# A decoder block on one core: x also read transposed, mixer weights in pieces in their order of use, no transposes ahead of the first product

## The reference

```python
def reference(x, p, positions, g_mix_norm, w_in, ...):
    h = rms_norm(x, g_mix_norm[i])
    proj = h @ w_in[i]
    q, k, v, g_ret, u_pool, gate_a, gate_b = jnp.split(proj, ...)
    qh = rotary(q.reshape(B, S, RET_HEADS, RET_HEAD_DIM), positions)
    kh = rotary(k.reshape(...), positions) * (RET_HEAD_DIM ** -0.5)
    ret = retention_chunkwise(qh, kh, vh)
    ...
    merged = jax.nn.sigmoid(gate_a) * branch_a + jax.nn.sigmoid(gate_b) * branch_b
    x = x + merged @ w_out[i]
    h2 = rms_norm(x, g_ffn_norm[i])
    x = x + moe(h2, w_router[i], b_router[i], w_gate_up[i], b_gate_up[i], w_down[i], b_down[i])
    h3 = rms_norm(x, g_ple_norm[i])
    ple_gate = jax.nn.sigmoid(h3 @ w_ple_gate[i])
    x = x + ple_gate * (p[i].astype(x.dtype) @ w_ple_proj[i])
    return rms_norm(x, g_final)
```

## Time and profile before

| | before |
|---|---|
| median of 3 runs | 1224.1 us (1223.71 to 1224.15) |
| span of the profiled execution, first to last instruction | 1221.4 us |
| TensorE busy | 1143.5 us, 94% |
| VectorE busy | 392.4 us, 32% |
| ScalarE busy | 202.4 us, 17% |
| moved by DMA | 457.25 MB, mean 374 GB/s |
| chain that ended last | TensorE 62%, DMA 33%, VectorE 3% |

### The profile page before, as it was taken

How to read it: one execution, slowest core, us unless ns; L and a number is a source line. 1 busy time by engine, 2 the same in 40 slices (tenths; PEclk the granted TensorE clock), 3 DMA queues, 4 the chain that set the end, 5 groups by cost and what they waited for, 6 DMA issues and landing times.

```text
span 1221.4 us, 12440 instructions
## 1 busy us (share of the span) xinstructions
PE 1143.5 (94%) x5360; PEld 588.4 (48%) x5361; DVE 392.4 (32%) x619; ACT 202.4 (17%) x273; POOL 8.4 (1%) x19
## 2 busy tenths in 40 slices
PE   7999999999999999989898988989999779989887
PEld 6788888874344343424342434343443344343336
DVE  6964765641132121303030403131302121221226
ACT  6464545430000010101010101010100000000115
POOL 0000010000000000000000000000000000000000
PEclk9999999999999999999999999999999989999999
DMA  9855345898999999999999999999999999999990
GB/s 346 317 173 170 114 168 206 357 427 367 399 420 427 428 428 428 428 429 428 427 427 428 428 423 428 428 427 427 427 428 428 429 425 427 427 429 425 421 372 35
DMA packets 57500, 457.25 MB, mean 374 GB/s; under 512 B 5466, under 2 KB 6874, under 8 KB 30370
## 3 DMA queue, kind: packets, MB, share of 16 engines
q1 hardware_dynamic: 55632, 453.26, 89.7%
q10 hardware_dynamic: 1810, 3.14, 0.8%
HBM read 455.34 MB, written 1.05 MB: 374 GB/s over the span
## 4 chain that ended last, share of the span: by engine, by line
PE 62%; DMA 33%; DVE 3%; issue 1%; ACT 0%; SPq 0%; DVEq 0%; ACTq 0%; POOLq 0%; POOL 0%
PE ps L674 61%; DMA ring<-in_w_down 27%; DMA ring<-in_w_gate_up 5%; DVE w_split L1481 1%; PE ps L681 1%; PE ps L982 0%; DMA const<-in_const 0%; PE ps L999 0%; DVE over_xn L1489 0%; SPq L627 0%; DVE ring L1773 0%; DVE ring L1536 0%; DVE B L1719 0%; DVE B L1723 0%; DVE B L1720 0%
## 5 line engine op out<-in xcount | busy, mean ns | idle before, releaser
L674 PE MATMUL ps<-ring,B 128*64 128x512 f32 (+1 forms) x2976 | 659.4, 597 | 50.3 <-DMA ring<-in_w_gate_up 34.2
L674 PEld LDWEIGHTS ps<-ring,B 128*64 128x64 f32 (+1 forms) x2976 | 226.7, 140 | 468.3 <-issue 463.7
L1719 DVE TENSOR_SCALAR B<-ps 128x1024 f32<-128x1024 f32 x16 | 19.6, 1225 | 462.1 <-PE ps L982 379.7
L674 PE MATMUL ps<-w_split,over_BhT 128*128 128x512 f32 x480 | 152.3, 393 | 0.9 <-DVE ring L1540 0.8
L1481 DVE TENSOR_TENSOR w_split<-ring,w_split 128x1024 fp32r<-128x1024 f32 x87 | 104.7, 1223 | 67.8 <-ACT w_split L1224 67.3
L1224 ACT CAST w_split<-ring 128x1024 fp32r<-128x1024 f32 x87 | 90.4, 1052 | 101.6 <-PE ps L674 99.0
L674 PE MATMUL ps<-w_split,over_xn 128*128 128x512 f32 x256 | 100.0, 390 | 0.0
L674 PEld LDWEIGHTS ps<-w_split,over_BhT 128*128 128x128 f32 x480 | 90.0, 189 | 19.9 <-DVE ring L1540 1.2
L1350 ACT COPY B<-ps 128x512 f32<-128x512 f32 x28 | 15.0, 588 | 508.4 <-PE ps L982 508.4
L674 PE MATMUL ps<-const,xn 128*128 128x128 f32 x512 | 61.6, 279 | 4.1 <-DVE const L1688 3.6
L674 PEld LDWEIGHTS ps<-const,xn 128*128 128x128 f32 x512 | 60.0, 196 | 6.8 <-issue 6.8
(11 more groups left out here) (166 smaller groups left out, 495.4 us busy)
## 6 DMA issues: line engine op xcount, KB each, us to landing
ring<-in_w_gate_up SPq DMA_DIRECT2D x118, 2048.0 KB, 32.4
ring<-in_w_down SPq DMA_DIRECT2D x56, 2048.0 KB, 31.8
ring<-in_w_in SPq DMA_DIRECT2D x28, 1024.0 KB, 5.4
ring<-in_w_gate_up SPq DMA_DIRECT2D x18, 1024.0 KB, 11.5
ring<-in_w_down SPq DMA_DIRECT2D x16, 1024.0 KB, 25.5
ring<-in_w_branch SPq DMA_DIRECT2D x8, 1024.0 KB, 6.9
ring<-in_w_out SPq DMA_DIRECT2D x4, 1024.0 KB, 5.0
ring<-in_w_ple_gate SPq DMA_DIRECT2D x4, 1024.0 KB, 19.9
```

Of the source, the lines that this page charges most:

```text
L674: return pe.matmul(out, lhsT, rhs, start=start, stop=stop, skip_group_check=True)
L1719: step(ve.tensor_scalar(gate, two_banks(0), LIMIT, None, ALU.min))
```

## The change

- x is handed over a second time, already transposed (`in_xT`, laid out as 128 partitions x 8 column blocks x 256 tokens), and loaded in four parts of 256 KB into the buffer B3. `high_x` and `low_x` make the two parts of hT from it in SBUF; the transposes of x and the banks that they filled are gone.
- `vectors` is handed over as 50 columns of 128 rows, loaded straight into `vecs`; the transposes and copies of the vectors are gone. The cast of the positions moves behind the low part of piece 5.
- The mixer's weights and the gate's come as one tensor `in_mixer` of 45 chunks, each laid out as its slot is, so that a chunk is 8 KB in a row per partition where it was four runs of 2 KB. Chunk 0 comes in two halves, between the parts of xT.
- x itself, which is still needed for the norm and the residual, is loaded behind chunk 2.
- For the first piece, TensorE goes through both token tiles column by column of h, with a wait for each ingredient (`first_products`).
- VectorE clears a block of 128x128 and TensorE multiplies it by itself eight times into an otherwise idle bank before the first product.

```diff
+            load_xT(0)
+            sp.dma_start(ring[:, 0, 0:PIECE], t["mixer"][0, :, 0:PIECE]).then_inc(first_half_loaded, 16)
+            load_xT(1)
+            sp.dma_start(ring[:, 0, PIECE:], t["mixer"][0, :, PIECE:]).then_inc(mixer_loaded[0], 16)
+            load_xT(2)
+            load_xT(3)
+            for c in range(1, 3):
+                load(c)
             for i in range(TILES):
                 sp.dma_start(x[:, i, :], t["x"][0, i * P:(i + 1) * P, :]).then_inc(x_loaded[i], 16)
-
-            w_in = t["w_in"][0].rearrange("(k p) n -> p k n", p=P)
...
+            for c in range(3, MIXER_CHUNKS):
+                load(c)
...
-            pe.wait_ge(early_loaded, 16)
-
-            pe.wait_ge(vec_loaded, 16)
-            pe.transpose(ps[:, 0, 0:5 * KD], vec_rows, ident[0:5 * KD, 0:5 * KD])
...
-            for i in range(TILES):
-                pe.wait_ge(x_loaded[i], 16)
-            for j in range(4):
-                transpose_bank(x, 4 + j, j, xT_psum)
+            pe.wait_ge(blank_ready, 1)
+            for _ in range(WARM_UP):
+                mm(ps[:, 6, 0:P], blank, blank, True, True)
...
+            e.wait_ge(vec_loaded, 16)
+            e.wait_ge(xT_or_gate_loaded[0], 16)
+            high_x(0)
             piece_loaded(e, 0)
             nc.scalar.copy(split_of(0)[:, 0, 0:N], piece_of(0)[:, 0:N]).then_inc(first_hi, 1)
+            high_x(1)
             nc.scalar.copy(split_of(0)[:, 0, N:], piece_of(0)[:, N:]).then_inc(hi_ready, 1)
             split[0] = 1
             for part in range(1, PARTS):
-                high(hT_parts, xT_psum, 0, G_MIX, hT_hi, 4, range(2 * part, 2 * part + 2))
+                e.wait_ge(xT_or_gate_loaded[part], 16)
+                for c in (2 * part, 2 * part + 1):
+                    high_x(c)
+                if part == 1:
+                    e.wait_ge(mixer_loaded[0], 16)
                 split_hi(part + 1)
...
             split_lo(ahead(-1))
+            step(ve.tensor_copy(pos, pos_int))
+            dve.wait_ge(early_loaded, 16)
...
-            w_gate = t["w_ple_gate"][0].rearrange("(k p) n -> p k n", p=P)
...
+            for at, unit in enumerate(PLE_RAW):
+                sp.wait_ge(used, RING.raw_free[at])
+                sp.dma_start(ring[:, unit, :], t["mixer"][MIXER_CHUNKS + at]).then_inc(xT_or_gate_loaded[at], 16)
```

More of the change, by code:

```diff
@@ L327, in build @@
         more = ExpertSemaphores(sem, "more")
+        more.pair_done, more.order = sem("more_pair_done"), sem("more_order")
         used = first.chunk_used
@@ L333, in build @@
         last_rows = sem("last_rows")
-        gate_loaded = [sem(f"gate_loaded{i}") for i in range(len(PLE_RAW))]
+        xT_or_gate_loaded = [sem(f"xT_or_gate_loaded{i}") for i in range(PARTS)]
         block = ctx.enter_context(nc.Block())
@@ L503, in load, with load_xT @@
                         sp.wait_ge(lo_ready, 2 * (former - (former > POOL_CHUNK)) + 2)
-                dst = ring[:, c % MIXER_SLOTS, :].rearrange("p (k n) -> p k n", k=k)
-                sp.dma_start(dst, src).then_inc(mixer_loaded[c % MIXER_SLOTS], 16)
+                sp.dma_start(ring[:, c % MIXER_SLOTS, :], t["mixer"][c]).then_inc(mixer_loaded[c % MIXER_SLOTS], 16)
+            def load_xT(part):
+                sp.dma_start(xT[:, 2 * part:2 * part + 2, :], t["xT"][:, 2 * part:2 * part + 2, :]).then_inc(xT_or_gate_loaded[part], 16)
+            load_xT(0)
[6 more added lines that the diff above has]
+                load(c)
             for i in range(TILES):
                 sp.dma_start(x[:, i, :], t["x"][0, i * P:(i + 1) * P, :]).then_inc(x_loaded[i], 16)
-            w_in = t["w_in"][0].rearrange("(k p) n -> p k n", p=P)
[L511 to L529, removed]
+            for c in range(3, MIXER_CHUNKS):
+                load(c)
             def load_fine(unit):
@@ L691, in transpose16, with products @@
                     transpose_bank(src, 4 + j, j, done)
-            def products(piece, part, i, parts, n_bank, halves=None):
+            def products(piece, part, i, parts, n_bank):
                 hi, lo = parts
@@ L1491, in low, with low_x @@
                                                  ALU.mult, ALU.subtract), done)
-            low(hT_parts, G_MIX, hT_hi, 0, hT_ready, 4, range(0, 2))
-            for columns, after, done in ((slice(0, N), first_hi, first_lo), (slice(N, 2 * N), hi_ready, lo_ready)):
+            def low_x(c):
+                dve.wait_ge(hT_hi, c + 1)
+                post(ve.scalar_tensor_tensor(hT_parts[1][:, c, :], xT[:, c, :], vecs[:, G_MIX + c:G_MIX + c + 1],
+                                             hT_parts[0][:, c, :].bitcast(F32), ALU.mult, ALU.subtract), hT_ready)
+            for c, after, done in ((0, first_hi, first_lo), (1, hi_ready, lo_ready)):
+                columns = slice(c * N, (c + 1) * N)
+                low_x(c)
                 dve.wait_ge(after, 1)
@@ L1499, in _ @@
             for part in range(1, PARTS):
-                low(hT_parts, G_MIX, hT_hi, 0, hT_ready, 4, range(2 * part, 2 * part + 2))
+                for c in (2 * part, 2 * part + 1):
+                    low_x(c)
                 split_lo(part + 1)
             split_lo(ahead(-1))
+            step(ve.tensor_copy(pos, pos_int))
+            dve.wait_ge(early_loaded, 16)
             for i in range(TILES):
@@ new lines, in vectors, with chunks, halves @@
+    words[:, G_HG:G_HG + KD] = by_row.transpose(1, 0, 2).reshape(P, KD)
+    words[:, POSITIONS:] = np.asarray(inputs["positions"][0], np.int32).reshape(TILES, P).T
+    return words.view(np.float32)
+def chunks(inputs):
+    import numpy as np
+    def halves(w, columns):
+        block = w.reshape(2, KD // 2, P, -1)[:, :, :, columns]
+        return [half.transpose(1, 0, 2).reshape(P, SLOT) for half in block]
+    w_in, w_branch, w_out, w_gate = (np.asarray(inputs[n][0]) for n in ("w_in", "w_branch", "w_out", "w_ple_gate"))
+    made = []
+    for j, cb in enumerate(COLUMN_BLOCKS):
+        if j == POOL_AFTER:
+            made.append(np.asarray(inputs["w_pool"][0]).reshape(KD, P, SEQ).transpose(1, 0, 2).reshape(P, SLOT))
+        made += halves(w_in, slice(cb * N, (cb + 1) * N))
+    width = [slice(n * N, (n + 1) * N) for n in range(2)]
+    for unit in range(4):
+        made += halves(w_branch[1 - unit % 2], width[unit // 2])
+    by_width = [halves(w_out, width[n]) for n in range(2)]
+    made += [by_width[n][half] for half in range(2) for n in range(2)]
+    assert len(made) == MIXER_CHUNKS
+    for n in range(2):
+        made += halves(w_gate, width[n])
+    return np.ascontiguousarray(np.stack(made))
@@ L1928 @@
     arrays = {f"in_{n}": np.ascontiguousarray(inputs[n]) for n in _INS}
-    arrays["in_const"], arrays["in_vectors"] = constants(), vectors(inputs)
+    arrays["in_const"], arrays["in_vectors"], arrays["in_mixer"] = constants(), vectors(inputs), chunks(inputs)
+    arrays["in_xT"] = np.ascontiguousarray(inputs["x"][0].T.reshape(KD, P, SEQ).transpose(1, 0, 2))
     tensors = {n[3:]: nc.dram_tensor(n, a.shape, mybir.dt.from_np(a.dtype), kind="ExternalInput").ap()
```

103 lines of the change are left out of this document (48 added, 55 removed).

## The result

| | before | after |
|---|---|---|
| median of ten executions | 1223.74 us (1222.96 to 1224.15) | 1226.95 us (1226.41 to 1228.60) |
| span of the profiled execution | 1221.4 us | 1225.0 us |
| T2 in the profiled execution | 34.84 us | 38.22 us |
| span less T2 | 1186.6 us | 1186.8 us |
| first product | 10.96 us | 7.13 us |

A forecast was written before the change was run, and what follows sets the result against it. The opening's chain through VectorE to T2 was taken as the bound, with chunk 4 just in time. T2 0.5 us later and nothing elsewhere made the span 1221.9, plus 2.7 gave 1224.6 us; range 1221.2 to 1227.8.

The forecast's parts named there:

- T2: Moment VectorE has read column block 0 and TensorE then runs without a gap; forecast to move from 34.84 to about 35.3.
- The forecast's own band: Opening: chunk 4 decides, having been only just in time with a megabyte now ahead; 1223.4 to 1225.9 us, chance 0.42.
- the slower rival: Opening: x starves and TensorE's clock falls at T2; 1226.3 us, with the clock 1228.0; chance 0.22.
- First product at 6.1: TensorE's start: first product at about 6.1 us, 4.8 us earlier, after the first half chunk lands and is cast.
- Blanks 1.8 to 3.7 us from 1.1: TensorE's opening: eight blank matmuls take 1.8 to 3.7 us from about 1.1 us, over before 6.1, costing nothing.
- x at 21.5, scaling at 24.7: Opening: x lands at 21.5 us, between bounds 16.8 and 23.8; VectorE scales sine and cosine at 24.7, before 24.84.
- the rival in which x starves: Part of the slower rival: x lands at 23.8, scaling at 27.0 instead of 24.84, T2 2.2 us later, 1226.3 us.
- The other half of that rival, the clock: TensorE idle 3.6 us before T2, so its clock falls there and adds 1.7 us: 1228.0 us.
- Chunk 4 at 28.1: SP's queue: chunk 4 lands at 28.1 instead of 26.4 us, 2.65 later for x less four times 0.23.
- the rival on the other side: The faster rival: larger packets also fill the biases' slow stretch, giving back 1.0 us, 1223.6 us; chance 0.26 overall.
- No gain by larger packets: SP's queue: larger packets bring no rate, chunk 4 at 29.05, T2 1.4 us later, 1225.5 us; chance 0.1.
- Faster: the DMA keeps up: Opening loads: chunk 4 before 26 us; 1223.6, or 1223.0 down to 1219.3 if VectorE's own work decides; chance 0.26.

The follow-up runs named there:

- f4: Changed kernel with xT in one load and chunk 0 in one load, in place of six pieces: 1227.29 us, ratio 1.0026.
- e5: Kernel before with only the mixer's weights handed over as one tensor in 8 KB rows; x and its transposes as before: 1225.23 us, ratio 1.001.
- e2: Changed kernel with only the expert biases issued after the cosine, the large constants left in place: 1223.46 us, ratio 0.9999.
- e1: Changed kernel with both large constants and expert biases issued on ScalarE's queue after the cosine: 1224.43 us, ratio 1.0008.
- f1: Changed kernel with constants and biases issued behind the cast of piece 9, and VectorE's angles computed between the low parts of pieces 2 to 5: 1220.83 us, ratio 0.9975.
- f2: Changed kernel with VectorE's angles computed between the low parts of pieces 2 to 5, constants and biases where they were: 1226.99 us, ratio 1.0026.
- f3: Changed kernel with WARM_UP at 0, leaving out the eight blank matmuls: 1226.62 us, ratio 1.0023.

## Why the prediction was right, and where it was wrong

The forecast was no change, 1224.6 us; it came out slower, 1226.95, inside the range but past the 2.4 us that I had set as the border, by 0.8 us. **The mechanism held; the size of one term did not.** The move was forecast as 0.5 us and came as 3.2, 2.7 more. In the time itself less of that shows, since the base of 1224.1 was 0.36 above the median of ten; it is not the span plus 2.7 either, for in every execution listed the time is 1.76 to 1.95 above its span.

*The range.* The forecast's own band, 1223.4 to 1225.9, was missed by 1 us. The range took the result in only because it was drawn wide for the slower rival, whose mechanism did not come about: in so far the hit was luck.

*What counts is T2.* Right: the table above. The first product 3.8 us earlier, the blanks and the rest of the mixer left no trace in the end.

*First product at 6.1.* It came at 7.13. The opening moved 0.37 MB less from 3 to 9 us than before (two windows of 280 and 356 GB/s). It cost nothing here, as TensorE had slack. Ahead of chunk 4 stand five more issues of SP and not two, and it is issued at 6.53 instead of 5.5; with the DMA share at 0.97 and 1.02 from 3 to 9 us no cost of that shows.

*Blanks 1.8 to 3.7 us from 1.1.* 3.78 from 1.03, the upper bound.

*x at 21.5, scaling at 24.7.* 21.41 and 24.66. The guess between 16.8 and 23.8 was good, and with it fell the rival in which x starves. The other half of that rival, the clock, fell too: TensorE's idle 3.64 us before piece 6 did lower the granted clock (0.77 on average from 29.8 to 37.2 us), but pieces 6 and 7 still ended 1.08 us before T2, and at T2 the clock was 1.00.

*Chunk 4 at 28.1.* **This is the term that failed**: it landed at 30.84, 2.7 us later. From there on the forecast's own steps hold: 7.2 us from landing to T2 were forecast, 7.4 came. What I had left out, each priced at 424 GB/s:

- The divided opening: 0.37 MB less from 3 to 9 us, 0.9 us. That it goes with the division is shown by f4.
- The stretch of the biases: 0.92 MB less than at 424 GB/s, 2.2 us, where before it was 0.52 MB less than at 388, 1.3 us: 0.9 us more. That this needs no second x is shown by e5. I had priced it only as a gain, in the rival on the other side.
- Bytes that went ahead: 0.93 MB of later chunks before the last byte of chunk 4, where I had kept the 0.35 of before: 0.58 MB, 1.4 us. It stands in e2 too (8.25 MB of SP's queue had moved when chunk 4 landed at 27.5), so it isn't the work of the biases; by f4 and e5 (0.40 and 0.30 MB) it goes with the division of the opening, not with the larger rows. What makes the packets of one load lag so far behind those of the next was not found.

These are 3.2 us, 0.5 more than the miss; by subtraction, the larger rows gave that much beyond the 0.92 us that I had credited them with. One sum checks the whole: by the landing of chunk 4, 10.57 MB had moved instead of 8.97, 1.60 MB more at the same mean rate; nearly all of it x (1.05) and the bytes that went ahead (0.58). At 340 GB/s 1.60 MB are 4.7 us, and chunk 4 was 4.4 later. No run moved x alone, so its share is by bytes and not by a test.

*No gain by larger packets* was the rival that came nearest (chunk 4 at 29.05, 1225.5). It is right for the sum over the opening, 340 against 343 GB/s, but not for its reason: the rows are faster, and other losses eat it. The Trainium skill, "DMA: Bandwidth & Descriptors", section "Why small descriptors are slow", would have given, as an estimate, 3% for the larger rows. This trace does not agree with it: 427 against 388 GB/s from 9 to 12 us are 10%. None of the losses above was in the forecast's price of the rows, 424 against 388 GB/s.

*Faster: the DMA keeps up.* It needed chunk 4 before 26 us. That is what e1 and f1 make true, and f1's 1220.83 lies where this rival stood, between 1219.3 and 1223.6.

## What to carry to other kernels

Where a start has to wait for a queue that is already just in time, moving the first work forward pays only if the bytes ahead of the last needed load become fewer too: find the load that the chain passes through, and list what stands before it on every queue, the other engines' small loads among it. An edit that is worth nothing while another thing binds can pay once that is gone, so try them together before dropping either. Price a landing by what the queues move per stretch, not by one good rate.

## What was not expected of the hardware

While the two loads of 256 KB into 32 partitions each are on their way, all queues together move 178 to 336 GB/s at a DMA share of 0.90 to 1.09, in each of the twelve profiles and wherever the loads are issued. Two megabytes in loads of 256 and 512 KB moved at 280 to 356 GB/s from 3 to 9 us, the same bytes in two loads at 407 to 423; and behind the divided loads more of the next chunks went ahead of the last byte of chunk 4, 0.51 to 0.93 MB against 0.30 to 0.40.

And the blanks do not keep the clock up. With them, TensorE idle for 2.28 us before the first product, the granted clock from 9 to 12 us was 0.50 (1.2 GHz) in f2, while in f3, which has none, it was 1.00. In the changed kernel's own profile it was 1.00 too, after 2.33 us of idling. The durations tell it otherwise than the granted clock: the first four products took 2.04 us in the changed kernel and in f3, and 1.38 us in f2, ahead of its stretch at 0.50. What decides it these runs don't show; T2 was 38.27 in f2 and 38.22 in the changed kernel.
